# Value products with high part and remainder side by side as one stationary operand

## The reference

```python
sc = jnp.where(kpos[None, :] <= qpos[:, None], sc, NEG)
p = jax.nn.softmax(sc, axis=-1).astype(v.dtype)
return jnp.einsum('bhqk,bhkd->bhqd', p, v)
```

## Time and profile before

| what | value |
|---|---|
| median of 3 runs | 1209.78 us (1209.39 to 1211.22) |
| the profiled execution: time | 1211.46 us |
| the profiled execution: span, first to last instruction | 1209.7 us |
| TensorE busy | 1174.9 us, 97% of the span |
| VectorE busy | 803.0 us, 66% |
| ScalarE busy | 570.2 us, 47% |
| GpSimd busy | 205.8 us, 17% |
| TensorE's granted clock, mean | 0.997 of full |

### The profile page before, as it was taken

How to read it: one execution, slowest core, us unless ns; L and a number is a source line. 1 busy time by engine, 2 the same in 40 slices (tenths; PEclk the granted TensorE clock), 3 DMA queues, 4 the chain that set the end, 5 groups by cost and what they waited for, 6 DMA issues and landing times.

```text
span 1209.7 us, 15326 instructions
## 1 busy us (share of the span) xinstructions
PE 1174.9 (97%) x6026; PEld 996.1 (82%) x6026; DVE 803.0 (66%) x1056; ACT 570.2 (47%) x861; POOL 205.8 (17%) x196
## 2 busy tenths in 40 slices
PE   6999989999999999999999999999999999999997
PEld 5887878798888888888898877888988888888886
DVE  5699765677666666544759887648766666664463
ACT  4455474554434343434445635745544344443432
POOL 1385173110000000000016833702000000000000
PEclk9999999999999999999999999999999999999999
DMA  8233332533333333566632333245323233336563
GB/s 250 75 88 85 92 78 95 184 98 114 102 90 105 91 101 94 168 194 212 199 103 80 88 92 94 87 135 157 94 87 105 88 105 95 96 100 200 176 226 134
DMA packets 155034, 146.83 MB, mean 121 GB/s; under 512 B 4783, under 2 KB 135763, under 8 KB 154963
## 3 DMA queue, kind: packets, MB, share of 16 engines
q1 hardware_dynamic: 154384, 145.12, 39.6%
q10 hardware_dynamic: 579, 0.74, 0.2%
HBM read 139.54 MB, written 2.10 MB: 117 GB/s over the span
## 4 chain that ended last, share of the span: by engine, by line
PE 79%; DVE 9%; ACT 3%; POOL 3%; issue 3%; DMA 2%; POOLq 0%; ACTq 0%; DVEq 0%
PE ps L555 25%; PE ps L557 25%; PE ps L556 25%; DVE wsp L457 2%; DMA raw<-in_w_out 2%; POOL rms_r L963 1%; POOL cf_out L972 1%; PE ps L849 1%; DVE ps L1258 1%; ACT wsp L449 1%; DVE yt L1058 1%; PE ps L617 1%; DMA rows<-in_vectors 1%; DVE xs L1071 1%; DVE x L1062 1%
## 5 line engine op out<-in xcount | busy, mean ns | idle before, releaser
L555 PE MATMUL ps<-xn,wsp 128*128 128x512 f32 (+1 forms) x1120 | 412.5, 368 | 3.0 <-DVE xn L1078 2.9
L556 PE MATMUL ps<-xn,wsp 128*128 128x512 f32 (+1 forms) x1120 | 409.3, 365 | 0.0
L557 PE MATMUL ps<-xn,wsp 128*128 128x512 f32 (+1 forms) x1120 | 409.3, 365 | 0.0
L457 DVE TENSOR_TENSOR wsp<-raw,wsp 128x1024 fp32r<-128x1024 f32 (+2 forms) x250 | 307.1, 1232 | 150.8 <-ACT wsp L449 150.6
L449 ACT ACTIVATE wsp<-raw 128x1024 fp32r<-128x1024 f32 (+2 forms) x256 | 265.7, 1041 | 159.0 <-PE ps L557 102.2
L555 PEld LDWEIGHTS ps<-xn,wsp 128*128 128x128 f32 x1120 | 211.9, 189 | 38.7 <-DVE xn L1078 4.1
L557 PEld LDWEIGHTS ps<-xn,wsp 128*128 128x128 f32 x1120 | 211.9, 189 | 33.9
L556 PEld LDWEIGHTS ps<-xn,wsp 128*128 128x128 f32 x1120 | 212.0, 189 | 33.6 <-issue 0.5
L555 PE MATMUL ps<-wsp,hid 128*128 128x512 f32 (+1 forms) x488 | 190.6, 391 | 0.8 <-DVE wsp L457 0.8
L557 PE MATMUL ps<-wsp,hid 128*128 128x512 f32 (+1 forms) x488 | 189.2, 388 | 0.0
L556 PE MATMUL ps<-wsp,hid 128*128 128x512 f32 (+1 forms) x488 | 189.1, 388 | 0.0
(11 more groups left out here) (157 smaller groups left out, 1226.7 us busy)
## 6 DMA issues: line engine op xcount, KB each, us to landing
raw<-in_w_ffn_up SPq DMA_DIRECT2D x88, 512.0 KB, 3.8
raw<-in_w_ffn_down SPq DMA_DIRECT2D x88, 512.0 KB, 4.1
raw<-in_w_in SPq DMA_DIRECT2D x36, 512.0 KB, 3.9
raw<-in_w_out SPq DMA_DIRECT2D x32, 512.0 KB, 3.6
x<-in_x SPq DMA_DIRECT2D x4, 512.0 KB, 8.1
xn<-xn SPq DMA_DIRECT2D x8, 256.0 KB, 3.3
out_x<-x SPq DMA_DIRECT2D x4, 512.0 KB, 4.0
raw<-in_w_vkr SPq DMA_DIRECT2D x4, 432.0 KB, 3.6
```

The source lines that it names most:

```text
L457: eng.tensor_tensor(wsp[:, u % SPLIT, 1, 0:nk * n], raw[:, (l * NU + u) % RAW, 0:nk * n], fp(wsp[:, u % SPLIT, 0, 0:nk * n]), ALU.subtract ...
L555: pe.matmul(dst, a[0], b[0], start=start, stop=False, skip_group_check=True)
L556: pe.matmul(dst, a[0], b[1], start=False, stop=False, skip_group_check=True)
L557: return pe.matmul(dst, a[1], b[0], start=False, stop=stop, skip_group_check=True)
```

## The change

The values' tiles are laid out anew: for each key block and head the 64 columns of the high part and the 64 of the remainder stand side by side. One matmul with these 128 stationary columns gives the high part's product in PSUM rows 0 to 63 and the remainder's in rows 64 to 127. Two matmuls, one with the probabilities' high part and one with their remainder, take the place of three (and so remainder by remainder is computed too). Each head has columns of its own in the bank; bank 0 holds chunks 0 and 1 of both heads, bank 1 chunks 2 and 3.

The two row blocks must then be added. ScalarE copies rows 64 to 127 to SBUF (`pv_rests`), VectorE adds them to rows 0 to 63 for each head (`head_sum`, into `pv_sums`), once for the early and once for the late chunks. When a pair is complete, ScalarE copies the sum as high part and VectorE writes the remainder, now from SBUF. The value products move to 7, 9 and 11 steps after the pair's first unit, the even head before the odd one; the output projection's second early row moves by a step, and the loop is one step longer. The order, with the lines that only rename left out:

```diff
-    if g < G_UP:
-        return PV_BANKS[(g - G_PV) % 2]
...
-VALUES_AT = (3, 7, 8)
-PV_TAKEN = 9
-ATT_TAIL = TRAIL + 5
+VALUES_AT = (4, 6, 8)
+PV_TAKEN = (4, 8, 10)
+ATT_TAIL = TRAIL + 6
 OUT_HI, OUT_LO = (8, 11, 14), (9, 10, 12, 13, 15, 16)
-OUT_EARLY = {N_UNIT + 1: 0, N_UNIT + 2: 1}
+OUT_EARLY = {N_UNIT + 1: 0, N_UNIT + 3: 1}
...
-        vm = hid[:, VM:VM + 2, :, :].rearrange("p a b t -> p (a b t)").rearrange("p (s c d) -> p s c d", s=2, c=TC)
-        vl = hid[:, VL:VL + 2, :, :].rearrange("p a b t -> p (a b t)").rearrange("p (s c d) -> p s c d", s=2, c=TC)
+        def by_head(first):
+
+            return hid[:, first:first + 2, :, :].rearrange("p a b t -> p (a b t)")\
+                .rearrange("p (n s d) -> p n s d", n=TC * HEADS, s=2)
+
+        vm, vl = by_head(VM), by_head(VL)
+
+        def values_of(tile, half, s):
+
+            return tile[:, 2 * half * HEADS:2 * (half + 1) * HEADS, s, :].rearrange("p (c h) d -> p c h d", c=2)
...
+        pv_rests = [place(f"pv_rest{i}", [P, T], f32, slot(Y_SLOT["c"] + i)) for i in range(PAIRS)]
+        pv_sums = [place(f"pv_sum{i}", [P, T], f32, slot(Y_SLOT["c"] + i) + 4 * T) for i in range(PAIRS)]
...
+        pv_even = sem("pv_even")
+        pv_rest = sem("pv_rest")
+        pv_sum = sem("pv_sum")
...
+
+        def heads_at(src):
+            return src.rearrange("p c (h d) -> p c h d", d=DH)
...
-                    pe.matmul(ps[:, bank, :], ident_r[:, :], vm[:, 0, 0:2, :].rearrange("p c d -> p (c d)"),
+                    pe.matmul(ps[:, bank, :], ident_r[:, :], vm[:, 0:HEADS, :, :].rearrange("p h s d -> p (h s d)"),
...
                 def values(pair, part):
 
-                    g = G_PV + pair
+
+
                     if part < 2:
-                        pe.wait_ge(pt_ready, l * N_UNIT + STEPS * pair + (2, STEPS)[part])
-                    if part == 0:
-                        bank_free(l, g - 2 if pair >= 2 else (G_MR, G_MQ)[pair])
+                        pe.wait_ge(pt_ready, l * N_UNIT + STEPS * pair + (2, STEPS - 1)[part])
+                    else:
+                        pe.wait_ge(pt_ready, l * N_UNIT + STEPS * pair + STEPS)
+                    if pair == 0 and part < 2:
+                        bank_free(l, (G_MR, G_MQ)[part])
+                    elif pair and part < 2:
+                        pe.wait_ge(pv_sum, (l * PAIRS + pair) * 2 - (part == 0))
                     v = vm if pair < PAIRS // 2 else vl
-                    c0 = pair % 2 * P
-                    for i in ((1, 0), (1,), (0,))[part]:
-                        m = P if i else DH
+                    for i in ((0, 1), (0,), (1,))[part]:
+                        h = pair % 2 * 2 + i
                         for kc in range(4 if part else 2):
                             skip = P if kc == (3 if part else 1) else 0
-                            out_cols = slice((part > 0) * 2 * P + skip, ((part > 0) * 2 + 2) * P)
-                            probs = [pt_late[:, i, s, kc, skip:2 * P] if part else pt_early[:, i, s, 2 * kc * P:(2 + kc) * P]
-                                     for s in range(2)]
-                            last = product(ps[0:m, bank_of(g), out_cols], [v[:, s, kc, c0:c0 + m] for s in range(2)], probs,
-                                           kc == 0, skip > 0)
-                    if part == 0:
-                        last.then_inc(pv_early, 1)
-                    if part == 2:
-                        last.then_inc(group_done, 1)
+                            out_cols = slice(i * 2 * P + skip, (i + 1) * 2 * P)
+                            both = v[:, kc * HEADS + h, :, :].rearrange("p s d -> p (s d)")
+                            for s in range(2):
+                                probs = pt_late[:, i, s, kc, skip:2 * P] if part else pt_early[:, i, s, 2 * kc * P:(2 + kc) * P]
+                                last = pe.matmul(ps[:, PV_BANKS[part > 0], out_cols], both, probs, start=kc == 0 and s == 0,
+                                                 stop=skip > 0 and s == 1, skip_group_check=True)
+                    last.then_inc((pv_early, pv_even, group_done)[part], 1)
...
-                        dve.tensor_tensor(vm[:, 1, 2 * i:2 * i + 2, :], val_at(i, 0, GW),
-                                          fp(vm[:, 0, 2 * i:2 * i + 2, :]), ALU.subtract).then_inc(vm_ready, 1)
+                        dve.tensor_tensor(values_of(vm, i, 1), heads_at(val_at(i, 0, GW)), fp(values_of(vm, i, 0)),
+                                          ALU.subtract).then_inc(vm_ready, 1)
...
+
+                def head_sum(pair, i, late):
+
+                    cols = slice(i * 2 * P, (i + 1) * 2 * P)
+                    return dve.tensor_tensor(pv_sums[pair][DH * i:DH * i + DH, late * 2 * P:(late + 1) * 2 * P],
+                                             ps[0:DH, PV_BANKS[late], cols], pv_rests[pair][DH * late:DH * late + DH, cols],
+                                             ALU.add)
...
-                    pair, r = divmod(t - TRAIL - PV_TAKEN - 1, STEPS)
-                    if r == 0 and 0 <= pair < PAIRS:
-                        dst = hid[:, Y_SLOT["c"] + pair]
-                        dve.wait_ge(pv_hi, l * PAIRS + pair + 1)
-                        dve.tensor_tensor(dst[:, 1, :], ps[:, bank_of(G_PV + pair), :], fp(dst[:, 0, :]), ALU.subtract)\
-                           .then_inc(pv_ready, 1)
+                    for pair in range(PAIRS):
+                        rel = t - TRAIL - STEPS * pair
+                        if rel in (PV_TAKEN[0] + 1, PV_TAKEN[1] + 1):
+                            late = int(rel > PV_TAKEN[0] + 1)
+                            dve.wait_ge(pv_rest, (l * PAIRS + pair) * 2 + late + 1)
+                            head_sum(pair, 0, late)
+                            head_sum(pair, 1, late).then_inc(pv_sum, 1)
+                        if rel == PV_TAKEN[2] + 1:
+                            dst = hid[:, Y_SLOT["c"] + pair]
+                            dve.wait_ge(pv_hi, l * PAIRS + pair + 1)
+                            dve.tensor_tensor(dst[:, 1, :], pv_sums[pair][:, :], fp(dst[:, 0, :]), ALU.subtract)\
+                               .then_inc(pv_ready, 1)
...
-                        act.activation(vm[:, 0, 2 * i:2 * i + 2, :], val_at(i, 0, GW), ACT.Copy).then_inc(vm_hi, 1)
+                        act.activation(values_of(vm, i, 0), heads_at(val_at(i, 0, GW)), ACT.Copy).then_inc(vm_hi, 1)
...
+                        pair, part, i = unit(s)
                         if pair and part == 0:
                             act.wait_ge(pv_early, l * PAIRS + pair)
+                        elif pair and i == 0:
+                            act.wait_ge(pv_even, l * PAIRS + pair)
                         elif pair:
                             group_ready(G_PV + pair - 1, l)
...
-                    pair, r = divmod(t - TRAIL - PV_TAKEN, STEPS)
-                    if r == 0 and 0 <= pair < PAIRS:
-                        group_ready(G_PV + pair, l)
-                        if pair == 1:
-                            act.wait_ge(kr_placed, (l + 1) * 64)
-                        act.activation(hid[:, Y_SLOT["c"] + pair, 0, :], ps[:, bank_of(G_PV + pair), :], ACT.Copy)\
-                           .then_inc(pv_hi, 1)
+                    for pair in range(PAIRS):
+                        rel, y = t - TRAIL - STEPS * pair, Y_SLOT["c"] + pair
+                        if rel in PV_TAKEN[:2]:
+                            late = PV_TAKEN.index(rel)
+                            if late:
+                                group_ready(G_PV + pair, l)
+                            else:
+                                act.wait_ge(pv_early, l * PAIRS + pair + 1)
+                            if pair == 1:
+                                act.wait_ge(kr_placed, (l + 1) * 64)
+                            act.activation(pv_rests[pair][DH * late:DH * late + DH, :], ps[DH:P, PV_BANKS[late], :], ACT.Copy)\
+                               .then_inc(pv_rest, 1)
+                        if rel == PV_TAKEN[2]:
+                            act.wait_ge(pv_sum, (l * PAIRS + pair) * 2 + 2)
+                            act.activation(hid[:, y, 0, :], pv_sums[pair][:, :], ACT.Copy).then_inc(pv_hi, 1)
```

More of the change, by code:

```diff
@@ L1274, in _ @@
                     dve.wait_ge(vl_hi, l * 2 + half + 1)
-                    dve.tensor_tensor(vl[:, 1, 2 * half:2 * half + 2, :],
-                                      ps[:, bank_of(G_MV + half), :].rearrange("p (c d) -> p c d", c=2),
-                                      fp(vl[:, 0, 2 * half:2 * half + 2, :]), ALU.subtract).then_inc(vl_ready, 1)
+                    dve.tensor_tensor(values_of(vl, half, 1),
+                                      heads_at(ps[:, bank_of(G_MV + half), :].rearrange("p (c d) -> p c d", c=2)),
+                                      fp(values_of(vl, half, 0)), ALU.subtract).then_inc(vl_ready, 1)
                 group_ready(G_MR, l)
@@ L1585, in _ @@
                     group_ready(G_MV + half, l)
```

(8 more changed lines are left out.)

## The result

The changed kernel takes 1218.81 us, the median of 4 runs (1217.25 to 1219.25), the kernel before 1209.59 beside it: a ratio of 1.0072 (95%: 1.0059 to 1.0085). It is slower by about 8.7 us. Forecast were 1207.7 us, faster than before, in a range of 1203.0 to 1211.0: the measured time lies above the range, and on the other side of the kernel before. Of the profiled executions, 1217.25 us is the lowest of its kernel's four and 1211.46 above its kernel's median, so the traces differ by less (spans 1215.4 and 1209.7) than the medians.

What follows compares the result with a forecast made beforehand. The prediction took TensorE to bound the attention stage. Per layer 3.1 - 0.6 - 1.45 = 1.05 us, twice 2.1, took the median from 1209.78 to 1207.7 us; range 1203.0 to 1211.0.

Steps and rivals of the forecast that it cites:

- The stage laid out anew: Attention steps 6 to 29 laid out by engine in program order: last value product ends 3.1 us earlier per layer.
- 5.2 less work: Value products, two matmuls for three: TensorE saves 1.3 us a pair, 5.2 us a layer, the ceiling for TensorE alone.
- 2.1 and 0.6 more of gaps: Attention stage, per layer: 2.1 us of the saving lost to TensorE gaps, 0.6 to the subtraction slowed beside GpSimd.
- sign of gaps over 9 us: Attention stage: TensorE's gaps grow from 4.7 to about 7 us; prediction wrong if they exceed 9 or stay under 5.
- GpSimd without pause in steps 9 to 17: Attention stage: GpSimd makes most of TensorE's gaps, with 15.8 us of work in steps 9 to 17.
- The rival that ScalarE and VectorE become the bound: Attention stage: they hold 10.7 and 10.4 of 11.7 us; 1212.3 us in all; chance 0.20, of which 0.12 lose over 0.2%.
- A late part: Value products of a pair after the change: 0.89 us for each late part, 0.82 for part 0, 2.6 a pair.
- 1.2 us at one place: Step 12, part 0 no longer between scores and transposes: copy, exponential, reciprocal and scaling can start up to 1.2 us sooner.
- the tail: Behind output row 2: weight remainder waits for the last sums, 1.45 us later per layer; TensorE's wait grows from 0.17 to 1.6.
- the 0.3 more: VectorE's four additions: if each waits for all earlier instructions, the 0.08 us overlap is lost, 0.3 us more a pair.
- The 1.05 and 1.75 us: Behind output row 2: bounds given with additions of 0.2 or 0.56 us.
- the strided writing of the values: Stretch 50 to 150 us: 16 instructions write in strides of 64 elements, hidden behind TensorE; without cover 1.6 us.

Runs made afterwards that it cites:

- All gaps filled: Changed kernel with useless matmuls in TensorE's three long waits of a layer, ten at step 17, five at 23, two at 24: 1213.96 us, ratio 1.0031.
- the deferred kernel: Changed kernel with the last copy and subtraction of pairs 0 to 2 moved to steps 24/25, 26/27 and 27/28: 1207.09 us, ratio 0.9977.
- without any sums: Changed kernel without the copies of the lower rows and the additions, last subtraction from PSUM, last copy and subtraction a step earlier; output wrong: 1200.53 us, ratio 0.9922.
- the move alone: Kernel before, with its three products, and part 0 of the value products one step later (VALUES_AT 4 for 3): 1203.64 us, ratio 0.9946.
- the weights early in both: Fourth and fifth output weights split in the loop: changed kernel with deferred copies and subtractions, 1203.07 us, 0.9940; kernel before with part 0 a step later, 1202.63 us, 0.9925.
- the fourth weight early: Changed kernel with the fourth output weight split in the attention loop at steps 26 and 27, ahead of the last sums: 1213.01 us, ratio 1.0019.
- one gap filled: Changed kernel with ten useless matmuls at step 17, ahead of unit 14's transposes: 1216.10 us, ratio 1.0049.
- the early weight: Changed kernel with last copies and subtractions of pairs 0 to 2 deferred and the fourth output weight split in the loop: 1204.01 us, ratio 0.9939.

## Why the prediction was wrong

**The step that failed is "The stage laid out anew"**, by which the last value product was to end 3.1 us earlier, or 2.5 with the slowed subtraction, at about 200.9. ScalarE's copy behind that product, its first sign, starts at 205.90 instead of 203.42: 2.5 us later, and 5.0 off the forecast. Of that step's two terms, the gaps came out near the sum and TensorE's work did not. From 150 us to that copy, in the changed kernel and in the one with the last copies and subtractions deferred:

```profile
150.00:205.90 55.90, 48.08 (x329) 41.89 (x328) 38.81 (x98) 38.83 (x103) 32.49 (x41) 0.94 0.24 72
```

```profile
150.00:200.57 50.57, 45.54 (x328) 38.91 (x327) 37.59 (x98) 38.67 (x104) 32.39 (x41) 1.00 0.28 79
```

| 150 us to the last value product, first layer | TensorE busy | gaps | together |
|---|---|---|---|
| before | 48.7 | 4.7 | 53.4 |
| the forecast: 5.2 less work, 2.1 and 0.6 more of gaps | 43.5 | 7.4 | 50.9 |
| changed | 48.1 | 7.8 | 55.9 |
| last copies and subtractions deferred | 45.5 | 5.0 | 50.6 |

The term of 5.2 us of saved work measured 0.6. Of the 4.6 us between them, 2.6 are the slow clock (48.1 against 45.5 for the same work at 2.4 GHz), and 2.0 are the rest, of which some 1.4 are value products that stand further apart than priced (below). The gaps were 0.4 off, and by luck: they don't lie where the layout had put them, for the most part in GpSimd's work, but behind VectorE's order, and the prediction's sign of gaps over 9 us stayed silent.

Why the layout missed the long wait: its sum gave the subtraction beside GpSimd 1.3 us (0.7 + 0.6; 1.7 at most), and it took 1.80; and it carried that as a term of the sum, 0.6, instead of carrying it through the order. An instruction in front of a reciprocal delays the reciprocal, GpSimd's scaling and TensorE in full where each of them has nothing else to do: 1.12 us less of subtraction took 1.14 us from TensorE's wait. The whole wait there grew to 2.49 us. The 0.6 was argued from "only the rest of GpSimd's instruction lies beside it"; that rest was all of it but 0.04 us. The trace of before held what was wanted: L1134's 1668 ns, and ScalarE and VectorE at 9.7 and 8.0 us of 11.7.

**Nothing was said of the clock.** The text took 2.4 GHz as given. Around the wait it was 1.2 GHz in both layers, for 6.8 us each time. All gaps filled, the program is 5.0 us faster. That is a little under half of the error of 11.1 us (1218.81 less 1207.7). Both the wait and the fall go with VectorE's order: deferring alone removes 11.5 us. The time is then 1207.09, close to the forecast, but that is luck in part, as the table shows: 2.0 us more of work a layer than forecast, and 2.4 us less of gaps.

**The limiter was named wrongly.** "GpSimd without pause in steps 9 to 17" did not come: it waited 2.05 us for VectorE ahead of unit 14. ScalarE's and VectorE's queues set the pace. The rival that ScalarE and VectorE become the bound had the direction right and its size too small: it counted their busy time, 10.7 and 10.4 of 11.7 us, and most of the loss is not from busy time but from the order in which it stands.

**TensorE's ceiling was too high.** A late part was priced at 0.89 us between starts. The timeline of the deferred kernel, at full clock:

```profile
184.97 1.15 PE L890 MATMUL ps<-hid 128*128 128x256 f32 x8
185.96 0.51 PE L865 MATMUL ps<-ident,prob 128*128 128x128 f32 x3
```

It takes 0.99, and part 0 of a pair, priced at 0.82, takes 0.95 to 0.99: some 2.95 us a pair where 2.6 was forecast. Over the program TensorE's busy time, in the page's first part, falls from 1174.9 us to this in the same kernel:

```profile
PE 1168.4 (97%) x5930; PEld 987.7 (82%) x5930; DVE 816.7 (68%) x1088; ACT 580.8 (48%) x877; POOL 204.3 (17%) x196
```

That is 6.5 us less, not 10.4 (5.2 a layer), though busy time also counts the end of the last matmul ahead of each added gap. And most of even this is not to be had: without any sums, the layout is only 2.9 us ahead of the move alone, since the other engines have little to give, as the earlier trace rows said.

**What the move is worth was never asked.** The prediction treated it as part of the layout and worked out 1.2 us at one place. Alone it gives 6.5 us in the program. The change's gain stands in one number of `VALUES_AT`. With the last copies and subtractions out of the way and the tail as it is, the new layout costs more than it brings, 0.9977 against 0.9946 for the move alone; with the weights early in both, 0.9940 against 0.9925, the two can't be told apart.

**What held, and what did so in part.** The durations of the added instructions: 0.42 us for an addition where 0.43 was taken, 0.59 and 0.63 for the copies at a bound of 0.6. Their prices did not: the additions were priced at 0.35 between starts, for an overlap of 0.08 us that did not come. Two take 0.84 us and the next instruction starts 0.87 behind the first, so a pair costs 1.7 us and not 1.4, which is the 0.3 more that the prediction had named beside its sum. The copies were priced at 0.50; in the loop the next instruction starts 0.62 and 0.66 us behind them, so ScalarE gets 1.4 us a pair and not 1.0. The tail: a wait of 1.70 us where 1.6 was expected and 0.17 had been, 1.53 more against 1.45. (The 1.05 and 1.75 us beside it are bounds of the delay, not of the wait.) Splitting a weight ahead of the sums removes it, for 4.6 us in the program rather than 3.1 (twice 1.53). On the kernel before, two weights split early give 1.9 us with only 0.17 us of such a wait to remove, so that edit has a gain of its own: its trace has none of the 2.6 us that TensorE (L617) waits for VectorE's `xs` in the trace of before. 192 value matmuls, none on 64 stationary columns, the feed-forward stretch at 171.85 of 172.00 us, and the strided writing of the values without effect (99.13 us of 100) held as well.

**Contention.** The change shows it and one experiment sets it apart: the two subtractions beside GpSimd, one in each layer, take 1.80 and 1.82 us, and with GpSimd's work elsewhere all eight take 0.68 to 0.69. In both layers the slow one ends 0.55 us behind the end of GpSimd's instruction. The Trainium skill, GPSIMD Engine Reference, section Key points, says that GpSimd contends with VectorE's instructions that have two SBUF inputs, and the runs agree. The prediction cited that, and took 0.6 us where L1134 had shown 1.0.

**What stays open.** Why the clock falls around one wait and not around another of the same length at the same place. With the fourth weight early it does not fall around 2.50 us in the first layer and does in the second; with one gap filled it falls around 1.36 and 0.60 us in the first layer and not in the second. No run tells this apart. Nor was the clock's share separated from the gaps' by more than the filler matmuls, which take TensorE's time themselves; 5.0 us is what they give net. Of the 4.6 us of the early weight, the two traces show 3.7 as waits, 3.4 of them for weight remainders; the rest was not traced. Why the matmuls of a value part stand further apart than those in the earlier trace rows was not asked either.

## What to carry to other kernels

When a change adds work to an in-order engine, write down what stands behind each added instruction and who waits for that, and put the added work where nothing does: the same instructions in the same kernel cost 11.5 us more in one place than in another, the fall of the clock included. When a change moves work as well as replacing it, price and run the move alone first; here it was all of the gain that could be measured. Carry a contention through the order of the work, as a duration at its worst row, and not as a term of the sum. Where a forecast comes out right, compare its terms as well: here two of them were 2 us off and cancelled.

## What the runs showed of the hardware

TensorE's granted clock can fall to 1.2 GHz in the middle of a busy kernel. In these traces it did so around one wait of 2.5 us (three times, for 6.8 us each) and around or behind one of 1.35 to 1.37 us (four times, in four kernels, for 3.4 us each; in three of them a wait of 0.60 us comes next), and rose again in the middle of work without pause. What TensorE does meanwhile takes about twice as long (0.21 us for 256 columns instead of 0.12). The Trainium skill, TensorE: Matmul & The Clock Gate, section HAM oscillation, tells of such falls where groups of matmuls of about 2 us alternate with waits for loads of 3 to 5 us. Here the clock fell too (0.55 at 181 to 188 us), and the wait was shorter than those, 2.49 us. The same waits without a fall show that the wait alone doesn't decide it.

VectorE's 128x512 subtraction with both operands in SBUF takes 0.68 us alone and 1.80 us while GpSimd works on SBUF. The additions with one operand in PSUM keep to 0.42 us throughout, beside GpSimd too (those at 171.94 us lie beside its scaling from 171.57 to 172.61). ScalarE's copy of 64x512 from PSUM takes 0.593 us, and its copy of 128x512 0.60: half the rows save next to nothing.
